# Subtracting the low halves of the layer weights on VectorE instead of GpSimd

## The chip, the cores and the metric

The kernel runs on one core of a Trainium2 chip. Times are device microseconds (us) of one execution. Before the change the median of three runs is 2853.03 us (2852.99 to 2853.11).

## The reference, cut to what matters

The program is a first block (pooling mixer, dilated attention, a 32-expert MoE) and then a second block, which goes through two layers on 256 tokens of width 1024. Only the second block is touched. One layer of it is:

```
x = x + 0.5 * swiglu(rms_norm(x, ffa_norm), ffa_w_in, ffa_w_out)
h = rms_norm(x, mix_norm)
(c_q, c_kv, k_rope, g_q, g_k, g_v, g_b, g_a, g_z, m_qkv, gate_logits) = split_cols(h @ w_in)
o_mla  = mla_branch(...)     # low-rank projections, head norms, rope, causal attention
o_gdn  = gdn_branch(...)     # causal convolution, l2 norm, gated delta rule
o_moba = moba_branch(...)    # head norms, rope, attention
up = einsum('bsnw,nwd->bsnd', stack(o_mla, o_gdn, o_moba), w_branch)
x = x + sum(sigmoid(gate_logits) * up, over the 3 branches) @ w_out
x = x + 0.5 * swiglu(rms_norm(x, ffb_norm), ffb_w_in, ffb_w_out)
```

## The kernel before

**Split weights.** Each matmul of a layer with a weight is three matmuls (`mm3`, L504 to L506): high part times high part, and the two mixed products. The high part of a weight is its copy rounded to the type fp32r, the low part is the weight minus that copy. A layer has 54 steps (`STEPS`), with one unit of weights each, and a unit comes as two "halves" (one for the last output step of each FFN), 106 halves in a layer. A half is cut into two pieces, mostly of 128x1024 values. For each piece SyncE loads 512 KB into one of four raw buffers, ScalarE writes the high part (`hi_act`, L483), GpSimd the low part (`lo_pool`, L489), and then the raw buffer is free for the load four pieces later. High and low parts lie in three slots of a half each. So ScalarE can start on half i only when TensorE has read half i-3 (`half_read`), and TensorE starts a half when both its low pieces are written (`weights`, semaphore `weights_split`).

**Who goes in which order.** Every engine runs a program written out by hand. ScalarE calls `splits.ahead(step)` at chosen places: it makes the high parts up to the third half after that step, so it waits there until TensorE is through with the step. GpSimd had nothing else to do in a layer, and wrote each low part as soon as its high part was there. VectorE does norms, rope, softmax, gates and the gated delta rule.

**TensorE's order in a layer:** norm transposes (L259); FFN 0; norm transposes; MLA rows; gates 0; transposes of the MLA latents (L1695); up_proj; gates 1; gates 2; MLA attention (L309 transposes q and k, L318 scores); MoBA rows 0 to 2; gates 3; gates 4; branch 0; MoBA attention; gdn 0 to 2; z; gates 5; l2 sums (L755); branch 2; the delta rule (L745); branch 1; wout 0 and 1; norm transposes; FFN 1. gates, gdn, branch and FFN-in steps are 96 matmuls of 256 columns, 48 to a half.

**VectorE's lines that matter:** head norms (L644, L645, L205, L206, a square root by ScalarE on L212, L647, L650 twice) and rope (L662 to L667, once for q and once for k) stand before each of the two attentions. `norm2_dve`: L205, L206, ScalarE's square root, L553 twice, then four parts of L559 and four times L562. The MLA latents go through L1815 and L1817. The branches' products are L1612. The convolution is L913 and L915, the l2 norm L923, L926, L930, L933. The merge of the branches is L1843 and L1847. ScalarE frees the PSUM banks of the gates with L1027, those of q, k and v with L1756 to L1762, and makes the products' banks of attention readable with L355.

Of the kernel before, what the change touches and what calls it, by code (L numbers as in the profile page):

```python
# [423 lines left out]
class Splits:  # L424
# [5 lines left out]
    def ahead(self, step):  # L430

        upto = min(last_half_of(step) + SPLIT_SLOTS + 1, len(HALVES))
        for i in range(self.done, upto):
            self.emit(self.k, self.eng, i)
        self.done = max(self.done, upto)
# [50 lines left out]
def lo_pool(k, pool, i):  # L486
    for n, at in pieces(i):
        pool.wait_ge(k.sem("weights_hi"), n + 1)
        k.nc.gpsimd.tensor_tensor(k.w[1][i % SPLIT_SLOTS][:, at], k.raw[n % RAW_SLOTS][:, 0:at.stop - at.start],  # L489
                                  k.w[0][i % SPLIT_SLOTS][:, at], ALU.subtract).then_inc(k.sem("weights_split"), 1)  # L490
# [56 lines left out]
def norm2_dve(k, dve, link, n, gain, power):  # L547
# [4 lines left out]
    for t in range(NT):  # L552
        V_.tensor_scalar(k.h[:, t, :], k.x[:, t, :], st[:, t:t + 1], None, ALU.mult).then_inc(k.sem("h_ready"), 1)  # L553
    for half in range(2):
# [63 lines left out]
def ffn_dve(k, dve, n):  # L618
    nc = k.nc
    silu, prod = k.s(SILU_TMP, 2, 512), k.s(SILU_TMP + 1024, 2, 512)  # L620
    for kind, u in FFN_STEPS:
        if kind == "out":
            continue
        b, free = k.filled(dve, ("up", n, u))
# [260 lines left out]
def gdn_dve(k, dve, link):  # L885
# [21 lines left out]
    for i in range(3):  # L907
        k.evacuated(dve, ("raw", i, 0), ("raw", i, 1))
        for j in range(4):
# [8 lines left out]
            else:  # L918
                ins.then_inc(k.sem("conv_ready"), 1)
    for i in range(2):  # L920
# [3 lines left out]
    for b4 in range(4):  # L924
        b, free = k.filled(dve, ("l2", b4))
        V_.tensor_scalar(G.sq[:, 2 * b4:2 * b4 + 2, :], part(b, 2, S), EPS, None, ALU.add).then_inc(free, 1)  # L926
    for b4 in range(4):
# [17 lines left out]
    link(V_.tensor_copy(G.XT[:, :].rearrange("p t h n -> p (t h) n"), bc(k.c("ident").unsqueeze(1), [P, 8, P])))  # L945
    branch_dve(k, dve, 2)
# [710 lines left out]
def layer_body(k, dram, layer):  # L1657
# [9 lines left out]
    with nc.Block() as block:  # L1667
# [124 lines left out]
        def _(dve):  # L1792
# [3 lines left out]
            norm2_dve(k, dve, link, 0, k.lv("g_ffa"), 0)  # L1796
            ffn_dve(k, dve, 0)
            norm2_dve(k, dve, link, 1, k.lv("g_mix"), 1)
            k.evacuated(dve, ("mla", 0), ("mla", 1))
# [10 lines left out]
            ins.then_inc(k.sem("c_ready"), 1)  # L1810
            gain = k.lv("c_norm")
# [12 lines left out]
            dve.wait_ge(k.sem("k_rope"), 2)  # L1824
            k.evacuated(dve, *[(x, t, i) for t in range(NT) for x in ("q", "kv") for i in range(2)])
            head_norm_dve(k, dve, link, mla.qk, k.s(QKT, 32, MLA_D), MLA_D, (k.lv("q_norm"), k.lv("k_norm")), 3)
            rope_dve(k, dve, link, mla.qk, QKT, 64, 16, k.c("cos16"), k.c("sin16"), k.sem("qk_ready"))
            mask = lambda t, pair: bc(causal[:, (1 - t) * P:2 * P].unsqueeze(1), [P, 2, (t + 1) * P])
            attn_dve(k, dve, link, mla, MLA_D ** -0.5, mask)
            k.evacuated(dve, *[("moba", i, t) for i in range(3) for t in range(NT)])  # L1830
            head_norm_dve(k, dve, link, moba.qk, k.s(QKT, 32, MOBA_D), MOBA_D, (k.lv("moba_q"), k.lv("moba_k")), 4)
            rope_dve(k, dve, link, moba.qk, QKT, 0, 32, k.c("cos32"), k.c("sin32"), k.sem("qk_ready"))
            branch_dve(k, dve, 0)
            attn_dve(k, dve, link, moba, MOBA_D ** -0.5, mask)
            gdn_dve(k, dve, link)

            branches = gatesT.rearrange("p (n c) s -> p n c s", n=3)
            link(V_.tensor_tensor(comb, branches[:, 0], branches[:, 2], ALU.add))
            branch_dve(k, dve, 1)
# [8 lines left out]
            for v in range(2):  # L1848
                for t in range(NT):
# [4 lines left out]
            ffn_dve(k, dve, 1)  # L1854

        @block.gpsimd
        def _(pool):
            for i in range(len(HALVES)):
# [174 lines left out]
```

## Time and profile before

| | |
|---|---|
| median of 3 runs | 2853.03 us |
| span of the profiled execution | 2852.2 us (0.8 us under the median) |
| TensorE busy | 2534.9 us, 89% |
| VectorE busy | 973.9 us, 34% |
| ScalarE busy | 888.3 us, 31% |
| GpSimd busy | 1027.5 us, 36% |
| first block | about 0 to 1170 us |
| layers | about 1170 to 2004 us and 2004 to 2852 us |

The span is the profiler's, from the first to the last instruction; the page gives no other time of that execution. The two layers are alike: the same TensorE stretches of the first layer lie 843 us earlier with durations equal to about 0.2 us, but for the first steps of either FFN and the MLA rows (11.40 us there, 9.47 here). Places are named by their time in the second layer.

### The profile page before, as it was taken

How to read it: one execution, taken by the hardware profiler on the slowest of the kernel's cores; microseconds unless marked ns; L12 is line 12 of the kernel's file. 1: busy time of each engine (PE TensorE's matmuls, PEld its weight loads, DVE VectorE, ACT ScalarE, POOL GpSimd, SP SyncE). 2: the span in 40 equal slices, each digit the busy share in tenths (PEclk: the TensorE clock that was granted, in tenths of full speed). 3: DMA queues.
4: the chain of work that ended last, by engine and by line, in shares of the span. 5: the costliest groups of instructions: out<-in, count | busy, mean ns of one | idle time of the engine just before them, and what ended most of it. 6: DMA issues, size and time to landing. Idle time of an engine off the chain costs nothing. (4 is left out here: it accounts for less than half of the span.)

```text
span 2852.2 us, 37927 instructions
## 1 busy us (share of the span) xinstructions
PE 2534.9 (89%) x15142; PEld 1826.0 (64%) x15142; DVE 973.9 (34%) x1514; ACT 888.3 (31%) x1266; POOL 1027.5 (36%) x428
## 2 busy tenths in 40 slices
PE   8889999999999998799778976899799777986899
PEld 3544443434434343599767866899799767875898
DVE  0322121212222121311465775221211557774221
ACT  1311212111111211444344531343444444431342
POOL 0000000000000000488548521688688546522686
PEclk9889999999999999899889997999899888997999
DMA  8249999999999995455325320354455324311453
GB/s 333 97 180 428 429 428 428 429 428 429 427 430 427 430 428 243 134 185 185 133 68 170 103 75 30 132 185 157 161 186 185 123 86 136 119 60 40 153 187 138
DMA packets 94236, 650.66 MB, mean 228 GB/s; under 512 B 10448, under 2 KB 12416, under 8 KB 68128
## 3 DMA queue, kind: packets, MB, share of 16 engines
q1 hardware_dynamic: 94112, 648.94, 58.8%
q8 instruction: 86, 1.41, 0.2%
q14 instruction: 38, 0.31, 0.0%
HBM read 647.84 MB, written 1.06 MB: 228 GB/s over the span
## 5 line engine op out<-in xcount | busy, mean ns | idle before, releaser
L489 POOL TENSOR_TENSOR w_lo<-raw,w_hi 128x1024 fp32r<-128x1024 f32 (+3 forms) x424 | 1027.3, 2446 | 1807.5 <-ACT w_hi L483 1807.5
L1319 PE MATMUL bank<-ring,scratch 128*64 128x512 f32 x3072 | 686.1, 596 | 27.2 <-DMA ring<-in_expert_units 25.4
L483 ACT CAST w_hi<-raw 128x1024 fp32r<-128x1024 f32 (+3 forms) x424 | 419.8, 1038 | 672.0 <-PE bank L506 659.6
L504 PE MATMUL bank<-hT_hi,w_hi 128*128 128x256 f32 x1984 | 566.1, 285 | 18.6 <-ACT scratch L1762 9.5
L505 PE MATMUL bank<-hT_lo,w_hi 128*128 128x256 f32 x1984 | 565.0, 285 | 0.0
L506 PE MATMUL bank<-hT_hi,w_lo 128*128 128x256 f32 x1984 | 564.9, 285 | 0.0
L1319 PEld LDWEIGHTS bank<-ring,scratch 128*64 128x64 f32 x3072 | 209.7, 137 | 455.0 <-issue 386.7
L504 PEld LDWEIGHTS bank<-hT_hi,w_hi 128*128 128x128 f32 x1984 | 384.8, 194 | 21.6 <-issue 10.5
L505 PEld LDWEIGHTS bank<-hT_lo,w_hi 128*128 128x128 f32 x1984 | 384.8, 194 | 0.8
L506 PEld LDWEIGHTS bank<-hT_hi,w_lo 128*128 128x128 f32 x1984 | 384.5, 194 | 0.0
L1487 DVE TENSOR_TENSOR scratch<-bank,scratch 128x512 f32<-128x512 f32 x64 | 44.3, 692 | 605.0 <-PE bank L1333 601.1
L626 DVE TENSOR_TENSOR scratch<-scratch,bank 128x512 f32<-128x512 f32 x44 | 30.3, 688 | 539.2 <-ACT scratch L612 539.2
L504 PE MATMUL bank<-w_hi,act_hi 128*128 128x512 f32 (+1 forms) x376 | 147.2, 392 | 6.9 <-ACT scratch L1027 6.9
L505 PE MATMUL bank<-w_lo,act_hi 128*128 128x512 f32 (+1 forms) x376 | 147.1, 391 | 0.0
L506 PE MATMUL bank<-w_hi,act_lo 128*128 128x512 f32 (+1 forms) x376 | 146.7, 390 | 0.0
L1305 PEld LDWEIGHTS bank<-scratch,h_rows 128*128 128x128 f32 x1056 | 124.9, 194 | 27.5 <-issue 27.5
L1305 PE MATMUL bank<-scratch,h_rows 128*128 128x128 f32 x1056 | 133.8, 281 | 0.0
L745 PE MATMUL bank<-scratch 128*128 128x128 f32 x816 | 106.0, 293 | 26.2 <-DVE scratch L986 7.3
L745 PEld LDWEIGHTS bank<-scratch 128*128 128x128 f32 x816 | 102.4, 206 | 32.0 <-issue 18.0
L1388 ACT COPY scratch<-bank 128x512 f32<-128x512 f32 x64 | 37.5, 586 | 265.9 <-PE bank L1319 265.9
L1390 ACT ACTIVATE scratch<-scratch 128x256 f32<-128x256 f32 x64 | 26.7, 417 | 276.2 <-DVE scratch L1490 276.2
L629 DVE TENSOR_TENSOR act_lo<-scratch,act_hi 128x512 fp32r<-128x512 f32 x44 | 102.3, 2324 | 30.2 <-ACT act_hi L615 30.2
(263 smaller groups left out, 2832.8 us busy)
## 6 DMA issues: line engine op xcount, KB each, us to landing
ring<-in_expert_units SPq DMA_DIRECT2D x192, 2048.0 KB, 20.5
raw<-in_layer_units SPq DMA_DIRECT2D x408, 512.0 KB, 4.7
ring<-in_first_units SPq DMA_DIRECT2D x6, 2048.0 KB, 23.9
ring<-in_ple_units SPq DMA_DIRECT2D x2, 2048.0 KB, 9.9
raw<-in_layer_units SPq DMA_DIRECT2D x8, 424.0 KB, 3.4
raw<-in_layer_units SPq DMA_DIRECT2D x4, 384.0 KB, 3.2
const<-in_const SPq DMA_DIRECT2D x1, 1184.0 KB, 7.3
x_res<-in_x SPq DMA_DIRECT2D x1, 1024.0 KB, 4.9
```

The lines of the kernel that those rows point to most:

```text
L483: k.nc.scalar.copy(k.w[0][i % SPLIT_SLOTS][:, at], k.raw[n % RAW_SLOTS][:, 0:at.stop - at.start]).then_inc(k.sem("weights_hi"), 1)
L489: k.nc.gpsimd.tensor_tensor(k.w[1][i % SPLIT_SLOTS][:, at], k.raw[n % RAW_SLOTS][:, 0:at.stop - at.start], k.w[0][i % SPLIT_SLOTS][:, at], ...
L504: nc.tensor.matmul(out, lhsT[0], rhs[0], start=start, stop=False)
L505: nc.tensor.matmul(out, lhsT[0], rhs[1], start=False, stop=False)
L506: return nc.tensor.matmul(out, lhsT[1], rhs[0], start=False, stop=stop)
L626: nc.vector.tensor_tensor(prod[:, u % 2, :], silu[:, u % 2, :], b[:, :], ALU.mult).then_inc(free, 1)
L629: nc.vector.tensor_tensor(lo, prod[:, u % 2, :], hi, ALU.subtract).then_inc(k.sem("act_lo"), 1)
L745: last = nc.tensor.matmul(b[:, h * P:(h + 1) * P], lhsT[:, h, :], rhs[:, h, :], start=True, stop=True)
L1305: last = nc.tensor.matmul(b[:, j * P:(j + 1) * P], k.h[:, t, c * P:(c + 1) * P], sel[:, t, :], start=(t == 0), stop=(t == 1))
L1319: last = nc.tensor.matmul(b[g * SL:(g + 1) * SL, :], lhsT[:, c, :], w[:, c, g, :], start=start and c == 0, stop=stop and c == 3)
L1388: nc.scalar.copy(rows[:, half, :], b[:, :]).then_inc(free, 1)
L1487: V_.tensor_tensor(both, b[:, :].rearrange("p (a n) -> p a n", n=SL), bc(wide_bias, [P, 8, SL]), ALU.add)\
```

## The change

The function `lo_pool` becomes `lo_dve`: the same subtraction, with the same semaphores, as a VectorE instruction. The GpSimd program of the layer goes. Since VectorE has an order of its own, its low parts are put into it at chosen places with `splits.ahead`, as ScalarE's are. The matmuls, the loads and ScalarE's program stay as they were.

```diff
     def ahead(self, step):
 
-        upto = min(last_half_of(step) + SPLIT_SLOTS + 1, len(HALVES))
+        self.to(last_half_of(step) + SPLIT_SLOTS + 1)
+
+    def to(self, end):
+
+        upto = min(end, len(HALVES))
         for i in range(self.done, upto):
             self.emit(self.k, self.eng, i)
         self.done = max(self.done, upto)
...
-def lo_pool(k, pool, i):
+def lo_dve(k, dve, i):
     for n, at in pieces(i):
-        pool.wait_ge(k.sem("weights_hi"), n + 1)
-        k.nc.gpsimd.tensor_tensor(k.w[1][i % SPLIT_SLOTS][:, at], k.raw[n % RAW_SLOTS][:, 0:at.stop - at.start],
+        dve.wait_ge(k.sem("weights_hi"), n + 1)
+        k.nc.vector.tensor_tensor(k.w[1][i % SPLIT_SLOTS][:, at], k.raw[n % RAW_SLOTS][:, 0:at.stop - at.start],
                                   k.w[0][i % SPLIT_SLOTS][:, at], ALU.subtract).then_inc(k.sem("weights_split"), 1)
...
         V_.tensor_scalar(k.h[:, t, :], k.x[:, t, :], st[:, t:t + 1], None, ALU.mult).then_inc(k.sem("h_ready"), 1)
+    between()
...
-def ffn_dve(k, dve, n):
+def ffn_dve(k, dve, n, splits):
...
         if kind == "out":
+            if u < FFN_OUT_UNITS - 1:
+                splits.ahead(STEP[f"ffn{n}", kind, u])
             continue
+        splits.ahead(STEP[f"ffn{n}", kind, u])
...
     for i in range(3):
+        splits.ahead(STEP["gdn", i])
         k.evacuated(dve, ("raw", i, 0), ("raw", i, 1))
...
+    splits.ahead(STEP["z", 0])
     for i in range(2):
         dve.wait_ge(k.sem("conv_silu"), i + 1)
...
         V_.tensor_scalar(G.sq[:, 2 * b4:2 * b4 + 2, :], part(b, 2, S), EPS, None, ALU.add).then_inc(free, 1)
+    splits.ahead(STEP["gates", 5])
...
     link(V_.tensor_copy(G.XT[:, :].rearrange("p t h n -> p (t h) n"), bc(k.c("ident").unsqueeze(1), [P, 8, P])))
+    splits.ahead(STEP["branch", 2])
     branch_dve(k, dve, 2)
...
+            splits = Splits(k, dve, lo_dve)
+            norm2_dve(k, dve, link, 0, k.lv("g_ffa"), 0, lambda: splits.to(1))
+            splits.to(SPLIT_SLOTS)
+            ffn_dve(k, dve, 0, splits)
             norm2_dve(k, dve, link, 1, k.lv("g_mix"), 1)
+            splits.ahead(STEP["ffn0", "out", 5])
+            splits.ahead(STEP["mla", 0])
...
             ins.then_inc(k.sem("c_ready"), 1)
+            splits.ahead(STEP["gates", 0])
...
+            splits.ahead(STEP["up_proj", 0])
             k.evacuated(dve, *[(x, t, i) for t in range(NT) for x in ("q", "kv") for i in range(2)])
             head_norm_dve(k, dve, link, mla.qk, k.s(QKT, 32, MLA_D), MLA_D, (k.lv("q_norm"), k.lv("k_norm")), 3)
+            splits.ahead(STEP["gates", 1])
             rope_dve(k, dve, link, mla.qk, QKT, 64, 16, k.c("cos16"), k.c("sin16"), k.sem("qk_ready"))
             mask = lambda t, pair: bc(causal[:, (1 - t) * P:2 * P].unsqueeze(1), [P, 2, (t + 1) * P])
+            splits.ahead(STEP["gates", 2])
             attn_dve(k, dve, link, mla, MLA_D ** -0.5, mask)
+            for i in range(3):
+                splits.ahead(STEP["moba", i])
             k.evacuated(dve, *[("moba", i, t) for i in range(3) for t in range(NT)])
             head_norm_dve(k, dve, link, moba.qk, k.s(QKT, 32, MOBA_D), MOBA_D, (k.lv("moba_q"), k.lv("moba_k")), 4)
+            splits.ahead(STEP["gates", 3])
             rope_dve(k, dve, link, moba.qk, QKT, 0, 32, k.c("cos32"), k.c("sin32"), k.sem("qk_ready"))
+            splits.ahead(STEP["gates", 4])
+            splits.ahead(STEP["branch", 0])
             branch_dve(k, dve, 0)
             attn_dve(k, dve, link, moba, MOBA_D ** -0.5, mask)
...
             link(V_.tensor_tensor(comb, branches[:, 0], branches[:, 2], ALU.add))
+            splits.ahead(STEP["branch", 1])
             branch_dve(k, dve, 1)
...
+                if v == 0:
+                    splits.ahead(STEP["wout", v])
...
             norm2_dve(k, dve, link, 2, k.lv("g_ffb"), 6)
+            splits.ahead(STEP["wout", 1])
+            ffn_dve(k, dve, 1, splits)
-
-        @block.gpsimd
-        def _(pool):
-            for i in range(len(HALVES)):
-                lo_pool(k, pool, i)
```

## Rows read from the trace of the kernel before

**Rows 1.** Busy time by stretch: us, then each engine's, clock, DMA; the mixing stretch

```profile
2215.00:2650.00 435.00, 340.98 (x2268) 310.72 (x2268) 265.38 (x323) 169.27 (x274) 201.77 (x81) 0.88 0.28 96
```

**Rows 2.** TensorE's waits in the second layer: us in total, times, longest

```profile
PE bank L309 <- DVE scratch L667: 26.4, 2, 14.1
...
PE bank L755 <- DVE scratch L923: 5.4, 1, 5.4
...
PE bank L504 <- ACT scratch L1027: 3.4, 1, 3.4
```

**Rows 3.** Costliest groups of the page: busy us, mean ns, idle before

```profile
L489 POOL TENSOR_TENSOR w_lo<-raw,w_hi 128x1024 fp32r<-128x1024 f32 (+3 forms) x424 | 1027.3, 2446 | 1807.5 <-ACT w_hi L483 1807.5
```

**Rows 4.** VectorE's groups by shape in the second layer

```profile
L629 DVE TENSOR_TENSOR act_lo<-scratch,act_hi 128x512 fp32r<-128x512 f32 x22 | 51.1, 2324 | 15.1 <-ACT act_hi L615 15.1
...
L923 DVE TENSOR_TENSOR scratch<-scratch 128x1024 f32<-128x1024 f32 x2 | 2.4, 1220 | 0.0
L1847 DVE TENSOR_TENSOR hT_lo<-scratch,hT_hi 128x512 fp32r<-128x512 f32 x4 | 2.5, 680 | 0.0
```

**Rows 5.** VectorE's timeline before MoBA attention: start, us, operation, idle before

```profile
2366.56 2.29 DVE L645 TENSOR_REDUCE scratch<-scratch 128x32 f32<-128x2048 f32 x1
...
2375.92 4.47 DVE L647 TENSOR_TENSOR scratch<-scratch 128x2048 f32<-128x2048 f32 x1 [4.33 <-ACT scratch L212]
...
2387.14 2.78 DVE L662 TENSOR_TENSOR scratch<-scratch,const 128x512 f32<-128x512 f32 x1
...
2403.82 0.69 DVE L662 TENSOR_TENSOR scratch<-scratch,const 128x512 f32<-128x512 f32 x1
...
2406.96 0.69 DVE L667 TENSOR_TENSOR scratch<-scratch 128x512 f32<-128x512 f32 x1
```

**Rows 6.** GpSimd's timeline in the same stretch

```profile
2379.30 23.94 POOL L489 TENSOR_TENSOR w_lo<-raw,w_hi 128x1024 fp32r<-128x1024 f32 x8 [1.05 <-ACT w_hi L483]
```

**Rows 7.** VectorE's timeline before MLA attention

```profile
2280.43 5.53 DVE L647 TENSOR_TENSOR scratch<-scratch 128x3072 f32<-128x3072 f32 x1 [5.37 <-ACT scratch L212]
...
2301.93 0.42 DVE L667 TENSOR_TENSOR scratch<-scratch 128x256 f32<-128x256 f32 x1
```

**Rows 8.** ScalarE's timeline: gates 2's banks freed before MLA attention

```profile
2290.27 1.08 ACT L1027 ACTIVATE scratch<-bank 128x512 f32<-128x512 f32 x2
```

**Rows 9.** Stretches with TensorE at either clock, columns as in Rows 1

```profile
2262.96:2268.90 5.94, 5.94 (x32) 5.94 (x33) 4.80 (x1) 1.00 (x4) 2.98 (x2) 0.59 0.65 228
2372.30:2395.35 23.05, 23.05 (x193) 22.84 (x191) 19.32 (x6) 12.74 (x15) 22.00 (x9) 1.00 0.54 179
```

**Rows 10.** DMA issues of the page: KB each, us to landing

```profile
raw<-in_layer_units SPq DMA_DIRECT2D x408, 512.0 KB, 4.7
```

**Rows 11.** VectorE's timeline at the start of the layer

```profile
2015.44 1.42 DVE L553 TENSOR_SCALAR h_rows<-x_res,scratch 128x1024 f32<-128x1024 f32 x2 [1.06 <-ACT scratch L212]
2017.40 0.69 DVE L559 TENSOR_TENSOR hT_hi<-bank,lvec 128x512 fp32r<-128x512 f32 x1 [0.54 <-PE bank L259]
```

**Rows 12.** VectorE's timeline after gates 0, around branch 2, the merge and norm 2

```profile
2245.75 0.56 DVE L1815 TENSOR_TENSOR act_hi<-bank,lvec 128x384 fp32r<-128x384 f32 x1 [3.47 <-PE bank L1695]
...
2504.37 12.98 DVE L930 RECIPROCAL scratch<-scratch 128x512 f32<-128x512 f32 x4
...
2525.13 2.49 DVE L1612 TENSOR_TENSOR scratch<-bank,scratch 128x512 f32<-128x512 f32 x4
...
2615.23 6.79 DVE L1843 TENSOR_TENSOR scratch<-scratch 128x512 f32<-128x512 f32 x4
...
2650.86 1.68 DVE L205 TENSOR_SCALAR scratch<-scratch 128x2 f32<-128x2 f32 x1 [3.42 <-ACT h_rows L233]
```

**Rows 13.** ScalarE's timeline at norm 1, after gates 0 and after the decay

```profile
2216.53 1.28 ACT L212 ACT_TABLE_LOAD   x1
...
2245.43 1.99 ACT L483 CAST w_hi<-raw 128x1024 fp32r<-128x1024 f32 x2 [4.19 <-PE bank L506]
...
2524.33 3.87 ACT L483 CAST w_hi<-raw 128x1024 fp32r<-128x1024 f32 x4
```

More of the change, by code:

```diff
@@ L542, in rows3_pe, with norm2_dve @@
             last.then_inc(k.sem("half_used"), 1)
-def norm2_dve(k, dve, link, n, gain, power):
+def norm2_dve(k, dve, link, n, gain, power, between=lambda: None):
     nc, st = k.nc, k.s(STATS, SCRATCH - STATS)
@@ L882, in gdn_act, with gdn_dve @@
         nc.scalar.copy(k.act2[0][:, 4:8, t * P:(t + 1) * P], part(b, 4, P)).then_inc(k.sem("go_hi"), 1)
-def gdn_dve(k, dve, link):
+def gdn_dve(k, dve, link, splits):
     nc, G = k.nc, Gdn(k)
@@ L1824, in _ @@
             dve.wait_ge(k.sem("k_rope"), 2)
+            splits.ahead(STEP["up_proj", 0])
             k.evacuated(dve, *[(x, t, i) for t in range(NT) for x in ("q", "kv") for i in range(2)])
             head_norm_dve(k, dve, link, mla.qk, k.s(QKT, 32, MLA_D), MLA_D, (k.lv("q_norm"), k.lv("k_norm")), 3)
+            splits.ahead(STEP["gates", 1])
             rope_dve(k, dve, link, mla.qk, QKT, 64, 16, k.c("cos16"), k.c("sin16"), k.sem("qk_ready"))
             mask = lambda t, pair: bc(causal[:, (1 - t) * P:2 * P].unsqueeze(1), [P, 2, (t + 1) * P])
+            splits.ahead(STEP["gates", 2])
             attn_dve(k, dve, link, mla, MLA_D ** -0.5, mask)
+            for i in range(3):
+                splits.ahead(STEP["moba", i])
             k.evacuated(dve, *[("moba", i, t) for i in range(3) for t in range(NT)])
             head_norm_dve(k, dve, link, moba.qk, k.s(QKT, 32, MOBA_D), MOBA_D, (k.lv("moba_q"), k.lv("moba_k")), 4)
+            splits.ahead(STEP["gates", 3])
             rope_dve(k, dve, link, moba.qk, QKT, 0, 32, k.c("cos32"), k.c("sin32"), k.sem("qk_ready"))
+            splits.ahead(STEP["gates", 4])
+            splits.ahead(STEP["branch", 0])
             branch_dve(k, dve, 0)
             attn_dve(k, dve, link, moba, MOBA_D ** -0.5, mask)
-            gdn_dve(k, dve, link)
+            gdn_dve(k, dve, link, splits)
             branches = gatesT.rearrange("p (n c) s -> p n c s", n=3)
             link(V_.tensor_tensor(comb, branches[:, 0], branches[:, 2], ALU.add))
+            splits.ahead(STEP["branch", 1])
             branch_dve(k, dve, 1)
@@ L1853, in _ @@
             norm2_dve(k, dve, link, 2, k.lv("g_ffb"), 6)
-            ffn_dve(k, dve, 1)
-        @block.gpsimd
-        def _(pool):
-            for i in range(len(HALVES)):
-                lo_pool(k, pool, i)
+            splits.ahead(STEP["wout", 1])
+            ffn_dve(k, dve, 1, splits)
     k.end_phase()
```

2 lines of the change are left out of this document (removed).

## The prediction

> **What bounds the kernel now.** I read the page first, then the busy time by stretch, the waits of TensorE, and the timelines of VectorE, ScalarE and GpSimd wherever TensorE stood still. TensorE sets the time. In the FFN stretches it never waits for a weight; in the mixing stretch of a layer it is busy for 341.0 of 435 us [rows 1], and what ends its longest pauses there is VectorE: 26.4 us of a layer wait for the rope that closes before the two attentions, 14.1 and so 12.3 us, then 5.4 us for the l2 squares [rows 2]. GpSimd is no bound by itself: it needs 2.446 us for a piece [rows 3], 4.9 us for a half, where a half of 48 matmuls takes 23.05 x 48/193 = 5.7 us [rows 9].
>
> But GpSimd slows VectorE. A rope multiply of 512 values takes 2.78 us while GpSimd works without a pause from 2379.30 to 2403.24, and 0.69 us at 2403.82 [rows 5, 6]. So do other operations with both inputs in SBUF: L647 with 2048 values takes 4.47 us where the one-input L645 with as many takes 2.29 [rows 5], and L629 takes 2.324 us for 512 values, where L1847 of the same shape and types takes 0.680 [rows 4]. These slow operations stand in the chains that TensorE waits for. The change removes GpSimd's work and so this excess. It adds 424 subtractions (two layers) to an engine with an order of its own, where a low part can be late, or the work behind it.
>
> **Prices.** The trace has no low part on VectorE. Below, it can't be under L1847's 0.680 us for half the values; above, it is 2.45 us if it cost what it does on GpSimd [rows 3, 4]. I take L923: 1024 values from SBUF, 1.22 us, the pair 2.35 [rows 4]; L1847 against 0.69 us in rope says that fp32r output costs nothing. A high pair is 1.99 us on ScalarE [rows 13], so after TensorE lets a slot go, the low pair ends 0.1 + 2.0 + 1.25 = about 3.4 us later on an idle VectorE (before: about 6). That keeps the FFN steps as they are: per step of two halves, 11.5 us, VectorE has two pairs and two small operations, some 6 us. The Trainium skill (VectorE: DVE Perf Modes, section on the TRN2 errata) has a table by which an fp32 operation of 1024 values takes 1.13 us; by that, an estimate, the nine or so pairs in the chains below would be 0.18 us shorter each, and the sum at the end 1.6 us lower per layer, 2848.4. The row of the trace decides, 1.22, and a second formula in that section gives the same.
>
> **Part by part, per layer** (plus is longer):
>
> - Layer start, +1.8. The first half's low pair stands between L553 and the first L559. It starts when L553 ends, 2016.86, ends at 2019.2, and L559 started at 2017.40 [rows 11]. TensorE waits for the third of the four parts that follow back to back.
> - Norm 1, -0.6; norm 2, -1.5. L205 took 1.68 us on 2 values beside GpSimd, and will take 0.17 as elsewhere. In norm 2 all of it shows [rows 12]; in norm 1 the square root's table load runs until 2217.81 anyway, and 0.6 is left [rows 13].
> - After gates 0, +2.3. The low pair of gates 1's first half is now ahead of L1815. Its high pair runs 2245.43 to 2247.42 [rows 13], the low pair ends at 2248.85, where L1815 started at 2245.75 [rows 12]: 3.1 later. TensorE waited for ScalarE's L1027 there in any case [rows 2], longer than for VectorE, which covers 0.8.
> - MLA rope, -4.2 before the clock. The square root comes at 2280.4 as before (ScalarE's order behind gates 1 sets it). From there L647 3.35, L650 2 x 1.7 (between 1024 and 2048 values): 2287.2. Then two low pairs until 2291.9, and rope 12 x 0.37 = 4.5: 2296.4, against 2302.35 [rows 7]. But TensorE needs the first of these pairs at 2282.6, for the second half of gates 2. It stands still for 7.0 us until 2289.7 and ends gates 2 at 2295.4, 7.1 late. Behind that wait are ScalarE's high pair for MoBA 1 (its raw buffers refill 4.7 us after the low pairs free them [rows 10], at 2295.4 and 2296.6) and then L1027, which frees the banks that attention needs first: it started at 2290.27 [rows 8] and will free the first bank at 2298.2. Attention starts at 2298.2 instead of 2302.4.
> - MoBA rope, -5.2 before the clock. The square root again comes as before, L647 at 2375.92 [rows 5]; 2.28 + 2.4 us bring the head norm to 2380.6. Two low pairs, 2385.3; rope 12 x 0.64 = 7.7, 2393.0 (before 2407.65 [rows 5]). TensorE wants gates 4's second half at 2378.1, gets it at 2383.0, wants branch 0's second half at 2394.5 and gets it at 2395.4. Branch 0 ends at 2401.2. Then gdn 1's first high pair and low pair (2404.5) stand before the L1612 quartet that frees the banks for k: 2407.0, the transposes end at 2407.8, and scores start at 2408.9, against 2414.1 now.
> - l2 and delta rule, +2.75. Two opposite terms. The convolution (two of three parts slowed) is no longer late, the 5.4 us wait [rows 2] goes; but two low pairs, 4.6 us, now stand before the reciprocals of 12.98 us [rows 12], and the sum there is only -2.2. After the decay, the low parts of the four high pieces of ScalarE (3.87 us, 2524.33 [rows 13]) come before L1612 at 2525.13 [rows 12]: the high ones now run from 2522.1 to 2526.0, the low ones follow from 2523.2, when VectorE's copies end, for 3 x 1.14 + 1.22 us, and L1612 starts at 2527.9. The chain behind it is one of latencies and moves whole.
> - Merge, +0.75. A low pair holds VectorE until 3.3 us after branch 1; then four L1612 (2.5, before mostly done while branch 1 ran) and L1843 in 2.5 instead of 6.79 [rows 12].
>
> The other places (MoBA rows, gdn steps, wout, FFN) cost nothing: the low pair is ready 3.4 us into a step of TensorE that lasts 11, and TensorE has a half or more in store; without that cover each would cost its 2.4 us. SyncE's loads wait for the low parts too. They start earlier than now where VectorE is free, and up to 7 us later in the two ropes, which is in the times above.
>
> **The clock.** TensorE resumes at half clock after each such pause: from 2262.96 the granted clock was 0.59 (between 1.2 and 2.4 GHz), 32 matmuls in 5.94 us where 3.8 would do, 2.1 lost [rows 9]. The new pauses of 7.0 and 4.9 us lie inside steps, so I charge 2.0 for MLA, 0.7 for MoBA (the 0.9 stall after it vanishes) and 0.5 after gates 0. The Trainium skill (TensorE: Matmul & The Clock Gate, section on HAM oscillation) has this as a rule that speaks against such a change: matmuls broken up by waits start slow again after each. The trace agrees, with 0.59 in that row.
>
> **Sum:** 1.8 - 0.6 - 1.5 + 2.3 - 4.2 - 5.2 + 2.75 + 0.75 = -3.9, with the clock +3.2: -0.7 per layer, -1.4 in all. The profiled span of 2852.2 us becomes 2850.8; the runs' median lies 0.8 above it, so 2851.6.
>
> **Rivals.** (1) Faster: the pauses are shorter or cost no clock, because high parts, loads and L1027 behind them come sooner than I chained them. With no clock term it is -3.9 per layer, 2845.2; with 1.5 us more from each rope, 2839. The overlap of operations and the bounds 0.68 to 2.45 allow it. (2) Slower: gates 2's late end. High pair, load and L1027 line up behind it, so that attention starts when it did, and MoBA likewise: the ropes' -9.4 + 2.7 go, +6.0 per layer, 2865. It decides when less than half of that gain (6.7) is left: then +2.6 per layer, 2858. Against it: L1027 has 4 us in hand. (3) A low part costs 2.4 us on VectorE too (L629's row read as the price of its types): about 1.2 us more for each of some 18 pieces in the chains, +21 per layer, 2893. L1847 speaks against it. (4) The change doesn't free VectorE: its slow operations have another cause. Then the low pairs come on top of the old chains, 4.7 us each at both ropes plus 9 elsewhere: about +18 per layer, 2889. The change from 2.8 to 0.69 us just when GpSimd stops speaks against it.
>
> **Chances.** Forecast, within 0.2% (5.7 us, about what a measurement tells from no change): 0.48. Rival 1: 0.28. Rival 2: 0.20. Rivals 3 and 4: 0.04. So faster 0.28, same 0.48, slower 0.24. The range reaches into rivals 1 and 2: 2841 to 2862; the forecast's own is 2847 to 2857.
>
> **What the profile would show.** Right: GpSimd empty after 1170 us; L489 on VectorE at 1.2 us; L662 to L667 at 0.4 and 0.7; L629 under 0.8; a TensorE pause of about 7 us in gates 2 and 5 us in gates 4, released by VectorE's low part; L309's pauses near 3 us and below; L755's pause gone; L1612 later after the decay. Wrong: a low part above 1.4 us, waits of TensorE for low parts in the FFN, or attention starting after 2302 minus the 1 us or so gained by then.

## The result and the profile after

The changed kernel took 2864.98 us (median of 5 runs, 2863.46 to 2866.44), the kernel before on the same chip 2853.11 us (2852.99 to 2855.46): a ratio of 1.004, 95% interval 1.0027 to 1.0052. It is slower, by more than the 0.2% that counts as no change, and outside the range of the prediction. In another set of runs, beside its own runs of the kernel before, it was 2863.46 us against 2854.37, ratio 1.0033 (1.0021 to 1.0046).

The page of the changed kernel: busy time of the engines, the costliest groups, the loads.

```profile
span 2863.1 us, 37969 instructions
...
PE 2561.6 (89%) x15142; PEld 1848.7 (65%) x15142; DVE 1238.8 (43%) x1938; ACT 891.4 (31%) x1266; POOL 0.2 (0%) x4
...
L493 DVE TENSOR_TENSOR w_lo<-raw,w_hi 128x1024 fp32r<-128x1024 f32 (+3 forms) x424 | 495.2, 1210 | 456.5 <-ACT w_hi L487 456.2
...
L508 PE MATMUL bank<-hT_hi,w_hi 128*128 128x256 f32 x1984 | 572.1, 288 | 46.3 <-DVE w_lo L493 24.7
...
raw<-in_layer_units SPq DMA_DIRECT2D x408, 512.0 KB, 4.9
```

GpSimd is empty, a low piece costs 1.21 us on VectorE, and VectorE is busy for 265 us more than before. TensorE is busy for 26.7 us more, with the same number of matmuls; its granted clock over the span is 0.936 instead of 0.942. The mixing stretch of the second layer, taken 7.7 us later here than in [rows 1], and TensorE's waits in it (in total, times, longest):

```profile
2222.70:2657.70 435.00, 352.80 (x2268) 321.14 (x2268) 279.68 (x401) 166.72 (x268) 0.00 (x0) 0.86 0.29 93
```

```profile
PE bank L508 <- DVE w_lo L493: 12.4, 2, 7.2
PE bank L508 <- DVE hT_lo L1873: 9.6, 1, 9.6
...
PE bank L753 <- DVE scratch L945: 5.0, 1, 5.0
...
PE bank L309 <- DVE scratch L1624: 3.0, 1, 3.0
PE bank L309 <- ACT scratch L1039: 3.0, 1, 3.0
```

The rope's 26.4 us of [rows 2] are gone and so are the 5.4 us of the l2 squares. In their place are two waits for a low part, 7.2 us in gates 2 and 5.1 in gates 4, and waits of 3.0 us at both attentions. VectorE's groups by shape in the second layer answer to [rows 4]:

```profile
L637 DVE TENSOR_TENSOR act_lo<-scratch,act_hi 128x512 fp32r<-128x512 f32 x22 | 15.2, 693 | 15.1 <-ACT act_hi L620 15.1
...
L933 DVE TENSOR_TENSOR scratch<-scratch 128x1024 f32<-128x1024 f32 x2 | 2.4, 1222 | 1.9 <-ACT scratch L867 1.9
...
L670 DVE TENSOR_TENSOR scratch<-scratch,const 128x512 f32<-128x512 f32 x2 | 1.4, 688 | 0.0
```

L637 is L629 of the kernel before, 0.693 us instead of 2.324. The rope operation that took 2.78 us beside GpSimd (L662 in [rows 5], L670 here) takes 0.69 us throughout; 1024 values from SBUF (L923, L933 here) take 1.22 us as before.

**Where the 10.9 us of span come from.** From the start of one TensorE stretch to the start of the next, second layer, changed minus before (us), beside the prediction's terms with its clock terms added where they fall (0.5 in up_proj, 2.0 and 0.7 in the two ropes):

| stretch | forecast | measured |
|---|---|---|
| layer start: transposes to FFN 0 | +1.8 | +1.65 |
| FFN 0 and norm 1 | -0.6 | -1.96 |
| norm 1's transposes to up_proj | +2.3 | +2.26 |
| up_proj to the end of MLA attention | -1.7 | -1.98 |
| MoBA rows to the end of MoBA attention | -4.5 | -0.94 |
| gdn steps to the first level of the delta rule | +2.75 | +2.94 |
| levels to wout | +0.75 | +0.87 |
| wout and norm 2 | -1.5 | -0.27 |
| FFN 1 and the end | 0 | +1.97 |
| **sum** | **-0.7** | **+4.54** |

The first layer is 3.9 us longer, and 2.5 us arise in the first block, before the layers. 3.9 + 4.5 + 2.5 = 10.9.

### The profile page after: what moved, and what is told of

It reads as the page before. It is cut to its first block and busy times, and to the rows that moved or that the text cites. A ratio compares the mean times of both kernels' runs of the same rounds, so it can differ in the third digit from the quotient of the medians.

```text
span 2863.1 us, 37969 instructions
## 1 busy us (share of the span) xinstructions
PE 2561.6 (89%) x15142; PEld 1848.7 (65%) x15142; DVE 1238.8 (43%) x1938; ACT 891.4 (31%) x1266; POOL 0.2 (0%) x4
## 5 line engine op out<-in xcount | busy, mean ns | idle before, releaser
L493 DVE TENSOR_TENSOR w_lo<-raw,w_hi 128x1024 fp32r<-128x1024 f32 (+3 forms) x424 | 495.2, 1210 | 456.5 <-ACT w_hi L487 456.2
L508 PE MATMUL bank<-hT_hi,w_hi 128*128 128x256 f32 x1984 | 572.1, 288 | 46.3 <-DVE w_lo L493 24.7
L1402 ACT ACTIVATE scratch<-scratch 128x256 f32<-128x256 f32 x64 | 26.7, 417 | 276.2 <-DVE scratch L1502 276.2
L508 PE MATMUL bank<-w_hi,hT_hi 128*128 128x512 f32 (+1 forms) x224 | 88.8, 396 | 22.2 <-DVE hT_lo L1873 19.2
L259 PE MATMUL bank<-const,h_rows 128*128 128x128 f32 x144 | 32.2, 416 | 77.4 <-DVE h_rows L557 53.0
```

The source lines that it names most:

```text
L259: last = nc.tensor.transpose(b[:, j * P:(j + 1) * P], k.h[:, t, c * P:(c + 1) * P], k.c("ident"))
L493: k.nc.vector.tensor_tensor(k.w[1][i % SPLIT_SLOTS][:, at], k.raw[n % RAW_SLOTS][:, 0:at.stop - at.start], k.w[0][i % SPLIT_SLOTS][:, at], ...
L508: nc.tensor.matmul(out, lhsT[0], rhs[0], start=start, stop=False)
L1402: nc.scalar.activation(sig[:, half], gu[:, half, :, 0:SL], ACT.Sigmoid, scale=ALPHA)\
```

## Why the attentions start so late

MLA attention first. VectorE's timeline, then ScalarE's, in the changed kernel (start, us, operation, idle before it and what ended it):

```profile
2289.22 3.36 DVE L655 TENSOR_TENSOR scratch<-scratch 128x3072 f32<-128x3072 f32 x1 [8.78 <-ACT scratch L212]
...
2296.20 4.63 DVE L493 TENSOR_TENSOR w_lo<-raw,w_hi 128x1024 fp32r<-128x1024 f32 x4
...
2304.81 0.42 DVE L675 TENSOR_TENSOR scratch<-scratch 128x256 f32<-128x256 f32 x1
```

```profile
2306.96 2.21 ACT L487 CAST w_hi<-raw 128x1024 fp32r<-128x1024 f32 x2 [1.45 <-DMA raw<-in_layer_units]
2309.07 1.08 ACT L1039 ACTIVATE scratch<-bank 128x512 f32<-128x512 f32 x2
```

The rope is through at 2305.2, but TensorE starts at 2309.80: the bank that it needs is freed by ScalarE's L1039, which stands behind a high pair, which waits for its load, which waited for the low pairs that were late. The pair isn't all of it: gates 2 ended only at 2306.80, behind the pause of 7.25 us in its middle, so without the pair L1039 could have started at most 2.3 us sooner. The same line forms before MoBA attention, and longer. VectorE, then ScalarE, then TensorE:

```profile
2387.16 4.63 DVE L493 TENSOR_TENSOR w_lo<-raw,w_hi 128x1024 fp32r<-128x1024 f32 x4
...
2399.31 4.62 DVE L493 TENSOR_TENSOR w_lo<-raw,w_hi 128x1024 fp32r<-128x1024 f32 x4
...
2411.50 2.44 DVE L493 TENSOR_TENSOR w_lo<-raw,w_hi 128x1024 fp32r<-128x1024 f32 x2 [2.03 <-ACT w_hi L487]
2413.85 2.48 DVE L1624 TENSOR_TENSOR scratch<-bank,scratch 128x512 f32<-128x512 f32 x4
```

```profile
2405.52 1.05 ACT L487 CAST w_hi<-raw 128x1024 fp32r<-128x1024 f32 x1 [4.22 <-DMA raw<-in_layer_units]
...
2410.42 1.05 ACT L487 CAST w_hi<-raw 128x1024 fp32r<-128x1024 f32 x1 [2.21 <-DMA raw<-in_layer_units]
...
2412.58 2.02 ACT L355 COPY scratch<-bank 64x512 f32<-64x512 f32 x4
```

```profile
2414.59 2.85 PE L309 MATMUL bank<-const,scratch 128*64 128x128 f32 x16 [3.04 <-DVE scratch L1624]
2418.31 10.58 PE L318 MATMUL bank<-scratch 64*128 64x128 f32 x32 [0.87 <-ACT scratch L355]
```

The two low pairs run until 2403.93, and each raw buffer is free only when its low piece ends, so ScalarE's high pieces come at 2405.52, 2407.16 and 2410.42, each after a wait for a load. VectorE's L1624, which frees the banks for the transposes, stands behind the last low pair, and ScalarE's eight L355, which the scores need, behind the last high pair. Then the 32 score matmuls run at the lower clock, in both layers. The clock of this and other stretches, changed kernel, then before (columns as in [rows 1]; the third value from the right is the granted clock):

```profile
2418.31:2428.89 10.58, 10.58 (x33) 8.62 (x34) 8.21 (x19) 6.68 (x25) 0.00 (x0) 0.50 0.04 16
...
2632.65:2657.22 24.57, 24.57 (x96) 19.77 (x96) 7.66 (x9) 6.01 (x6) 0.00 (x0) 0.89 0.26 85
2667.73:2716.01 48.28, 48.28 (x385) 48.28 (x386) 28.50 (x34) 18.83 (x21) 0.00 (x0) 0.95 0.58 186
```

```profile
2414.12:2419.59 5.47, 5.47 (x32) 4.67 (x32) 4.55 (x12) 4.42 (x18) 0.00 (x0) 1.00 0.01 1
2623.38:2646.71 23.33, 23.32 (x96) 18.87 (x96) 3.13 (x5) 6.01 (x6) 13.77 (x6) 0.94 0.31 105
2658.73:2705.04 46.31, 46.31 (x385) 46.31 (x386) 11.33 (x16) 18.70 (x21) 33.19 (x14) 1.00 0.44 143
```

The scores take 10.58 us at 0.50, the 1.2 GHz level, instead of 5.47 at 1.00; wout takes 1.24 us and the first part of FFN 1 1.97 us more, also at a lower mean clock. (In the first layer all of FFN 1 is only 0.8 us longer.)

The 5.1 us that the scores lose do not all reach the end of the attention. From their start to the next step (gdn 0) it takes 20.70 us in the changed kernel and 19.43 before, 1.27 more. Before, TensorE waited behind the scores for VectorE's softmax (L389), 0.47, 1.35, 1.26 and 1.10 us; in the changed kernel 1.00 us of such waits is left. The slow scores mostly fill time in which TensorE would have waited.

## Experiments

They ran in three sets, each beside runs of the kernel before on its own chip: 2854.65 us (median of 12 runs) for the first four, 2855.22 (21) for the next four, 2854.37 (16) for the last three. "After" stands for the changed kernel.

**1. The kernel before again.**

> The kernel before, unchanged, for a second profile. In the profile of the changed kernel the first block, which is not touched, ends 2.5 us later (the norm transposes of the first layer start at 1175.2 instead of 1172.7). If that is the scatter of the weight loads of the experts, two profiles of the same kernel differ there by some us too. If it belongs to the change, this profile shows 1172.7 again to within a few tenths.

Measured: 2853.65 us, span 2851.8; the transposes of the first layer start at 1172.8 us, 0.1 from the first profile. The trace of before repeats. By this expectation the 2.5 us would belong to the change; experiment 9 decides it the other way.

**2. The low pairs in the shadow of the head norms' square root.** VectorE waited 8.8 and 6.5 us there for ScalarE; the two low pairs now stand ahead of this wait.

```diff
 def rstd_dve(k, dve, link, v, mean, n, shadow=lambda: None):
...
     k.nc.vector.reciprocal(v, v).then_inc(k.sem("inverse_variance"), 1)
+    shadow()
...
-            head_norm_dve(..., 3)
-            splits.ahead(STEP["gates", 1])
+            head_norm_dve(..., 3, lambda: splits.ahead(STEP["gates", 1]))
```

and the same for `gates 3` in MoBA's head norm.

> Changed kernel, but the two low pairs that stood between head norm and rope are made while VectorE waits for the square root of the head norm, where it is idle for some 9 us. Theory 1 (place in VectorE's order): the pauses of 7.2 us in gates 2 and 5.1 us in gates 4 vanish, rope ends 4.7 us earlier in both, the gates keep 2.4 GHz; MLA attention starts about 9 us earlier and the MoBA scores about 8 us, some 17 to 22 us per layer: 2821 to 2831 us. Theory 2 (VectorE has 495 us more to do, wherever it stands, and TensorE's waits only move to another low part): less than 5 us in all, 2860 to 2865.

Measured: 2841.87 us, ratio 0.9953 (0.9940 to 0.9967). MLA attention starts 33.5 us behind up_proj's end instead of 42.6, and waits 3.6 us for the rope again. The stretch from the MoBA rows to the scores is 79.9 us against 84.0. MLA attention gains the 9 us expected, the MoBA scores 4 of the 8, and the whole is 23 us below after where 34 to 44 were expected. The reason is in TensorE's waits and in ScalarE's timeline:

```profile
PE bank L310 <- DVE scratch L1625: 4.7, 1, 4.7
PE bank L310 <- DVE scratch L676: 3.6, 1, 3.6
```

```profile
2389.77 1.04 ACT L488 CAST w_hi<-raw 128x1024 fp32r<-128x1024 f32 x1 [1.82 <-DMA raw<-in_layer_units]
...
2391.92 2.01 ACT L356 COPY scratch<-bank 64x512 f32<-64x512 f32 x4
```

The line of low pair, load, high pair and copies before MoBA attention is still there, with the scores at 10.58 us. The pauses inside gates 2 and 4, with what stands behind them, were worth 8.0 us per layer up to the end of MLA attention and 4.8 to 5.2 at MoBA, but they were not the only loss.

**3. TensorE kept busy in three pauses** (42, 56 and 38 products that nobody reads, before up_proj and before the second halves of gates 2 and 4).

```diff
+def keep_busy(k, pe, key, n):
+    k.evacuated(pe, key)
+    b, _ = k.uses.at[key]
+    for _ in range(n):
+        k.nc.tensor.matmul(k.bank[b][:, 0:S], k.hT2[0][:, 0, 0:P], k.hT2[0][:, 0, :], start=True, stop=True)
```

> Changed kernel, with added matmuls of 256 columns that nobody reads, put into three pauses of TensorE (42 after the latents' transposes, 56 before the second half of gates 2, 38 before that of gates 4), at 0.12 us each less than the pauses of 5.7, 7.2 and 5.1 us. Nothing else is changed. If the granted clock after a pause is what makes the change slower than forecast: up_proj falls from 9.4 to about 6.5 us, the half of gates 2 from 8.2 to 5.8, that of gates 4 from 8.0 to 5.8, 5 to 8 us per layer, 2849 to 2855 us. If the clock is beside the point: 2863 to 2867 us, since the pauses end when the low part is there.

Measured: 2861.88 us, ratio 1.0027 (1.0017 to 1.0038). up_proj takes 7.16 us (9.36 in after) and the halves behind the two pauses 6.01 and 6.02 us (8.2 and 8.7). So the three pauses cost 2.2 + 2.2 + 2.7 = 7.1 us of clock in the matmuls behind them in the second layer. But the layers are only 1.0 and 1.2 us shorter than in after. The time lies outside both expected ranges, 3.1 and 1.6 us under the two measurements of after, and the intervals of the ratios overlap. Up to the end of MoBA attention 2.5 of the 7.1 us arrive (3.5 in the first layer), and the stretch from the levels to wout, where nothing was edited, takes 2.7 us longer. TensorE's waits in the second layer:

```profile
PE bank L309 <- ACT scratch L1051: 5.3, 1, 5.3
PE bank L309 <- DVE scratch L1636: 4.8, 1, 4.8
```

These waits were 3.0 and 3.0 in after: TensorE arrives earlier and waits for ScalarE's and VectorE's line. Most of a pause's clock cost is hidden where another engine sets the next start.

**4. GpSimd busy again on its own data,** beside VectorE's low parts: the work of the change stays as it is, four subtractions of 256 values on GpSimd are added per high piece, and no one waits for them but the end.

```diff
+        @block.gpsimd
+        def _(pool):
+            link = chain_of(pool, k.sem("own_step"))
+            for n in range(2 * len(HALVES)):
+                pool.wait_ge(k.sem("weights_hi"), n + 1)
+                for _ in range(4):
+                    link(nc.gpsimd.tensor_tensor(k.fvec[:, 60:316], k.const[:, 0:256], k.const[:, 256:512], ALU.subtract))
```

> Changed kernel, with GpSimd busy again on values of its own: at each high piece it makes four subtractions of 256 values from constants into a table that the layers don't use. It shares no data with the rest and nobody waits for it. If GpSimd's work on SBUF is what made VectorE's operations with two SBUF inputs slow, they get slow again: rope of 512 values from 0.69 to more than 1.2 us, low parts from 1.21 to more than 1.8 us, and the time grows by more than 30 us, to over 2895. If the slowness had another cause, 2863 to 2867 us.

Measured: 3122.16 us, ratio 1.0932 (1.0911 to 1.0952). Of that, 72 us are GpSimd's own end: its work runs until 3116 us, TensorE's only until 3044, where it ended at 2857 in after. The rest is 187 us. It is no measure of what GpSimd cost before, since GpSimd is busy here for 1705.6 us and was for 1027.3. What bears on the question is VectorE's low part, whose data and order are unchanged:

```profile
L1891 POOL TENSOR_TENSOR fvec<-const 128x256 f32<-128x256 f32 x1696 | 1705.6, 1006 | 1410.3 <-ACT w_hi L487 1278.0
L493 DVE TENSOR_TENSOR w_lo<-raw,w_hi 128x1024 fp32r<-128x1024 f32 (+3 forms) x424 | 665.0, 1611 | 325.6 <-ACT w_hi L487 325.1
```

1.61 us in the mean against 1.21, and the rope multiply of 512 values (L670) 1.17 against 0.69. Both are slower, though not by as much as expected (over 1.8 and over 1.2). GpSimd's work slows VectorE's, as the prediction read it in [rows 5, 6], and rival 4 falls. The Trainium skill (SBUF — State Buffer, section on who interferes with whom) says that a VectorE instruction with two SBUF inputs contends with a GpSimd instruction that reads SBUF, and that one with at most one SBUF input doesn't, outside the modes in which it uses both ports, which copies and tensor_scalar can enter. These rows agree with it: the one-input reduction of 2048 values takes 2.29 us with GpSimd at work, here (L653) as in [rows 5] (L645), and 2.29 us in after, while the tensor_scalar L922 takes 0.88 us here and 0.35 in after.

**5. The low pair behind the latents.**

```diff
-            splits.ahead(STEP["gates", 0])
+            splits.to(last_half_of(STEP["gates", 0]) + SPLIT_SLOTS)
...                       (the latents' products)
+            splits.ahead(STEP["gates", 0])
```

> One place alone. The low pair of gates 1's first half goes behind the latent products, so that VectorE forms these as soon as gates 0 is through; only the pair of up_proj's second half stays ahead of them. If the pair standing ahead is what costs there (theory of order), the pause before the up projection goes from 5.66 us back to near 3.4 us and the up projection of 9.36 us to near 8.8 us: 2.8 us earlier in each layer, some 5.6 us in all, about 2859. The pause in gates 2 of 7.25 us stays or grows by what the lead was. Rival: the path behind it is held by ScalarE's high pieces and its copies of the banks, then attention starts when it did and nothing of the 2.8 us reaches the end: 2863 to 2866.

Measured: 2857.9 us, ratio 1.0009 (1.0000 to 1.0018). The pause before up_proj is 3.43 us and up_proj takes 8.75, as expected. Of TensorE's waits in the second layer the two that matter are both ScalarE's:

```profile
PE bank L508 <- ACT scratch L1039: 3.4, 1, 3.4
PE bank L309 <- ACT scratch L1039: 3.2, 1, 3.2
```

MLA attention starts 56.2 us behind the six transposes that follow gates 0 (58.4 in after): 2.2 of the 2.8 us arrive there. The layers are 1.8 and 3.5 us shorter in all, for other stretches moved too: in the second layer MoBA attention came out 2.9 us and FFN 1 2.0 us shorter, but the stretch from the levels of the delta rule to wout 2.5 us longer, none of which the edit touches. There the matmuls ran for 15.70 us at a granted clock of 0.54 behind the 320 of the levels, against 12.60 us at 0.68 (up to the matmuls of branch 1) in after.

**6. The low pairs around the delta rule moved off its chain.**

```diff
+    splits.to(last_half_of(STEP["gates", 5]) + SPLIT_SLOTS)
     for b4 in range(4):
+        if b4 == 2:
+            splits.ahead(STEP["gates", 5])
         b, free = k.filled(dve, ("l2", b4))
...
-    splits.ahead(STEP["gates", 5])
...
-    splits.ahead(STEP["branch", 2])
     branch_dve(k, dve, 2)
...                       (end of gdn_dve)
+    splits.ahead(STEP["branch", 2])
```

> The stretch from the l2 squares to the first level of the delta rule alone. The low pairs that stood ahead of the reciprocals and ahead of the copies of the branch product go behind them or between them. The stretch from the end of gates 5 to the first level took 44.67 us before and 47.61 us in the changed kernel. If the low pairs ahead of the chain are what costs (theory of order), 9.9 us of VectorE's work leave the chain in each layer: the stretch takes about 38 us, and the time is about 2845. Rival: ScalarE's part of the chain (its high pieces of 3.9 us and the decay) comes last, then the stretch takes 44 us or more and the time is 2858 or more.

Measured: 2845.73 us, ratio 0.9970 (0.9958 to 0.9981). From the end of gates 5 to the first level it takes 37.6 us (after 47.6, before 44.7; expected 38). VectorE's timeline in after, then in this kernel:

```profile
2503.38 4.62 DVE L493 TENSOR_TENSOR w_lo<-raw,w_hi 128x1024 fp32r<-128x1024 f32 x4
2507.92 12.98 DVE L941 RECIPROCAL scratch<-scratch 128x512 f32<-128x512 f32 x4
...
2529.01 4.63 DVE L493 TENSOR_TENSOR w_lo<-raw,w_hi 128x1024 fp32r<-128x1024 f32 x4 [0.37 <-ACT w_hi L487]
2533.56 2.48 DVE L1624 TENSOR_TENSOR scratch<-bank,scratch 128x512 f32<-128x512 f32 x4
```

```profile
2494.15 2.35 DVE L493 TENSOR_TENSOR w_lo<-raw,w_hi 128x1024 fp32r<-128x1024 f32 x2
...
2498.88 12.98 DVE L943 RECIPROCAL scratch<-scratch 128x512 f32<-128x512 f32 x4
...
2519.64 1.89 DVE L1626 TENSOR_TENSOR scratch<-bank,scratch 128x512 f32<-128x512 f32 x3
```

Both groups of four low pieces, 4.6 us each, stood in a chain of latencies, and the stretch is 10.0 us shorter in each layer, as expected. The median is 17.7 to 19.3 us under the two of after. The profiled execution, 2851.49 us and so 5.8 above the median, lost part of it again between the levels and wout, 2.7 us longer per layer, as in experiment 5.

**7. The branch products ahead of the low pairs** at MoBA attention (`branch_dve(k, dve, 0)` and `splits.ahead(STEP["branch", 0])` swapped on VectorE).

> Two lines swapped: VectorE forms the four branch products that free the banks for the k transposes of MoBA attention ahead of the low pair of branch 0's successor, not behind it. In the changed kernel TensorE pauses 3.04 us there and then takes 10.58 us for 32 score matmuls at the lower clock, where the kernel before took 5.48 us. If that pause is what lets the clock fall (theory of the clock), the pause goes to under 1 us, the scores take 5.5 to 8 us, and each layer gains 2 to 7 us: 2851 to 2861. Rival: the clock had fallen in the 5.11 us pause of gates 4 and does not come back in between; then the scores stay above 8 us, the gain is 0 to 2.4 us per layer, 2860 to 2865.

Measured: 2861.53 us, ratio 1.0025 (1.0014 to 1.0036). The pause before the transposes went, and one of 4.99 us came behind them, ended by ScalarE's L355; the scores stayed at 10.58 us and began 1.5 us earlier (82.6 us behind the rows). My theory that the pause at the transposes lets the clock fall is wrong as put: swapping VectorE's order only moves the pause, since the high pair ahead of L355 comes no sooner. The rival's range (2860 to 2865) held, but not its reason, that the clock doesn't come back after gates 4: the 32 transposes just before this pause ran in 3.65 us at a granted clock of 1.00.

**8. All placements together:** 2, 5, 6 and 7, and branch 1's low pair behind the merge.

> All placements together: low pairs in the shadow of the two head norms, behind the latents, behind the reciprocals and the decay, behind the branch products and behind the merge. The first of these alone measured 2841.9, 23 us under the changed kernel and 12.8 us under the kernel before on the same chip. If the places add up (theory of order), latents take 5.6 us, the delta stretch 19.8 us and the merge and the branch products some 3 to 8 us more from it: 2808 to 2814. Rival: what is taken from VectorE's order is then set by ScalarE or by the loads, and the places do not add: 2825 to 2840. Above 2842 the theory of order is wrong for all but the head norms.

Measured: 2797.71 us, ratio 0.9795 (0.9781 to 0.9808), lower than either theory had it. The places do add, 67 us below after (66 by its second measurement). Stretch by stretch of the second layer it is the sum of the single ones to about 1 us: -2.3 at the latents, -8.3 at MLA attention, -7.7 at MoBA attention (4.8 and 2.3 alone), -10.2 up to the levels. The rest is the pair at the merge, which was not tried alone: the pause before wout is 4.48 us instead of 9.62.

**9. The changed kernel again.**

> The changed kernel once more, for the scatter of its first block and a second profile. Theory: the extra 2.5 us of its first block (1175.2 us against 1172.6 to the first transposes of layer 1) belong to the expert loads and not to the change, since the four kernels that leave the first block alone showed 1173.2 to 1178.1; then the mixing stretches and the FFN repeat within 1 us and only the first block moves. The time comes to 2861 to 2866. Rival: the first block is again at 1175 or more and the time at 2865, as of an effect of the change.

Measured: 2863.46 us (2860.95 to 2869.46), span 2860.7. The first layer's transposes start at 1172.44 us (1175.18 in the first profile, 1172.65 in before). From there to those of the second layer 847.80 us (847.50; before 843.60), and from those to TensorE's end 833.93 (833.91; before 829.37). So the layers repeat to 0.3 us and their 8.4 to 8.8 us are the change's effect. The 2.5 us of the first block are not there again; the other kernels here that share after's first block had 1172.2 to 1178.1. It scatters from one execution to another, and I count it as that.

**10. One pair of each engine moved behind, before MoBA attention.** Only this, on after:

```diff
 ScalarE
-            splits.ahead(STEP["branch", 0])
-            attn_act(k, act, moba)
+            splits.to(last_half_of(STEP["branch", 0]) + SPLIT_SLOTS)
+            attn_act(k, act, moba, lambda: splits.ahead(STEP["branch", 0]))     (behind the eight L355)
 VectorE
-            splits.ahead(STEP["branch", 0])
             branch_dve(k, dve, 0)
-            attn_dve(k, dve, link, moba, MOBA_D ** -0.5, mask)
+            splits.to(last_half_of(STEP["branch", 0]) + SPLIT_SLOTS)
+            attn_dve(k, dve, link, moba, MOBA_D ** -0.5, mask, lambda: splits.ahead(STEP["branch", 0]))     (behind the softmax)
```

> The changed kernel with one pair of each engine moved: ScalarE makes the last high pair before MoBA attention behind its eight copies of the transposed q and k, and VectorE the low pair of it behind the softmax and the branch products ahead of it. In the changed kernel ScalarE's high pair at 2410.42 waits 2.21 us for its load and stands before these copies; the scores start at 2418.31, 84.04 us behind the start of the MoBA rows, and take 10.58 us. If the late low pair, the load behind it and the high pair behind that are what hold the scores (theory of the chain over three engines), the scores start some 80 us behind the rows and keep to 5.5 to 8 us: 4 to 9 us less per layer, 2848 to 2857. Rival: the copies are ready early but the clock is low anyway, 10.6 us for the scores, 2 to 4 us less per layer: 2857 to 2862.

Measured: 2853.17 us, ratio 0.9997 (0.9988 to 1.0006): no difference from the kernel before, 10 to 12 us below after. ScalarE and TensorE before the scores:

```profile
2404.96 3.96 ACT L355 COPY scratch<-bank 64x512 f32<-64x512 f32 x8 [1.74 <-PE bank L309]
2408.78 2.01 ACT L489 CAST w_hi<-raw 128x1024 fp32r<-128x1024 f32 x2
```

```profile
2404.32 3.65 PE L309 MATMUL bank<-const,scratch 128*64 128x128 f32 x32
2409.17 8.98 PE L318 MATMUL bank<-scratch 64*128 64x128 f32 x32 [1.19 <-ACT scratch L355]
```

The scores start 80.3 us behind the rows (84.0 in after, 80 expected) and take 8.98 us, a little over the 5.5 to 8 expected. From the rows to the end of this attention it is 98.7 us, against 104.7 in after and 105.7 before: 6.0 us for one pair on each engine, of which 3.8 are the earlier start of the scores. In the first layer it is 7.0 us, and the scores took 5.47 us there, behind the same pause:

```profile
1564.52 5.47 PE L318 MATMUL bank<-scratch 64*128 64x128 f32 x32 [1.19 <-ACT scratch L355]
```

**11. The same on top of all placements.**

> The same move on top of all the placements together, which measured 2797.7. There TensorE waited 4.85 us for ScalarE's first copy, and the scores took 10.57 us. By the chain over three engines the pause becomes about 1 us and the scores 5.5 us: 4 to 9 us less per layer, 2780 to 2790. Rival: the low pair behind the softmax comes too late for gdn 0's second half and gives it back: 2795 to 2802.

Measured: 2789.97 us, ratio 0.9775 (0.9762 to 0.9789). TensorE before the scores, in kernel 8 and then here:

```profile
2369.93 10.57 PE L319 MATMUL bank<-scratch 64*128 64x128 f32 x32 [4.85 <-ACT scratch L356]
```

```profile
2351.99 3.65 PE L310 MATMUL bank<-const,scratch 128*64 128x128 f32 x32
2356.83 5.47 PE L319 MATMUL bank<-scratch 64*128 64x128 f32 x32 [1.19 <-ACT scratch L356]
```

In the second layer both parts of what the line costs are gone: the pause is 1.19 us instead of 4.85, and the scores take 5.47 us instead of 10.57. In the first the scores still take 8.13 us:

```profile
1548.09 8.13 PE L319 MATMUL bank<-scratch 64*128 64x128 f32 x32 [1.47 <-ACT scratch L356]
```

That makes no difference to the end: the attention is over 18.8 us behind the start of the scores in the first layer and 18.9 in the second. With 10.57 us it was 21.2 and 19.7. This version is 2.25% faster than the kernel before and 2.6% faster than the change as made.

## Why the prediction was wrong

**The step that failed** is the MoBA rope, "-5.2 before the clock" with 0.7 for the clock. It was -0.94 instead of -4.5 by the end of that attention, 3.6 of the 5.2 us by which the second layer missed. It has two parts, 3.0 and 0.6 us:

- The line of engines. The prediction had "gdn 1's first high pair and low pair (2404.5)" ahead of the branch products, which end at 2407.0, and scores at 2408.9. The layer's part ahead of it runs 6.4 us later in after; less that, the low pair ended at 2407.5, the products at 2409.9 and the scores began at 2411.9, 3.0 late. Each raw buffer waits for a late low pair, and ScalarE then waited 4.22, 0.59 and 2.21 us for loads. I had named the mechanism for MLA and stopped short of pricing it here. This is the larger part: the sum let the last high and low pair follow at once, and had at nothing the waits for loads in front of them and the copies (L355) queued behind them.
- The clock. I took the scores to run at 2.4 GHz as before and even counted a stall as gone. They ran at 1.2 GHz, +5.1 us, of which 1.27 reached the end of the attention, since the softmax covers the rest; 0.7 was charged. Experiment 10 took out the pair that makes the line and had 6.0 us back, 3.8 by the earlier start and 2.2 within the attention.

**The clock elsewhere.** I charged 3.2 us per layer for it, at three pauses. Experiment 3 has 7.1 us of clock at these three, of which the 1.6 at up_proj were there before (8.75 us against 7.16): 5.5 are new. Too little charged, and yet not what moved the end, since little of what experiment 3 took away got there. What the forecast lacks are +1.97 us in FFN 1 and +1.24 in wout, and -1.3 in FFN 0. TensorE's pause before norm 2's transposes is 5.60 us in after and in experiments 5 and 6 alike, yet the first part of FFN 1 takes 48.28 us in the one and 46.31 in the other two. So these terms don't follow from the length of the pause; what they follow from no experiment shows, and they stay open.

**The total of rival 2.** Its 2865 us is what came. Its mechanism, "high pair, load and L1027 line up", is real at MLA attention, where the wait for L1039 (the same operation) comes last, but there the stretch still gained 1.98 us, where 1.7 was forecast. It decided at MoBA attention, and with other copies (L355 and not L1027). The chance of 0.20 was too low, since both ropes have the same line and I weighed only the first. And 2.5 us of the first measured time are the first block's scatter, so that the number agrees so well is luck.

**Right, term by term.** A low piece at 1.22 us (measured 1.221 for 1024 values); rival 3 falls. VectorE freed: L662's 2.78 us became 0.69 and L629's 2.324 became 0.693; experiment 4 puts the cause in GpSimd. Layer start +1.8 (1.65), latents +2.3 (2.26), the clock in up_proj +0.5 (0.62), delta rule +2.75 (2.94), merge +0.75 (0.87), norm 1 -0.6 (0.64). Norm 2's -1.5 was there (12.03 to 10.51 us) and was hidden by wout's clock. The pauses of 7.0 and 4.9 us in gates 2 and 4 were 7.25 and 5.11. MLA attention came right in part by luck: it started 1.6 us sooner behind up_proj's end, where 2.2 was forecast, and then was itself 1.0 us shorter, which the sum did not have.

The gain that a free VectorE offers was therefore there: experiments 2, 5, 6 and 10 each got some of it back by moving nothing but low or high pairs. The change lost it by placing low pairs (at MoBA attention a high pair of ScalarE's too, once it came late) ahead of the operation for which TensorE waits next.

## What to carry to other kernels

When work moves from a helper engine into the order of an engine on the critical path, each piece needs a place of its own: in the shadow of a wait that exists anyway, or behind the operation that TensorE needs next. One placement rule for all of them ("ahead of the next step") cost 75 us here against hand-picked places, one of them a high pair of ScalarE's. Where three engines feed a ring of buffers (load, high part, low part), follow a late piece once round the ring, load included, and through everything queued behind the next high part, before taking the gain of an earlier end for granted. And judge a placement by its own stretch, in both layers, and not by the total alone: the savings of the stretches added up to within about 1 us, while stretches that nobody touched moved by 2 to 3 us with the clock.

## What was not expected of the hardware

The clock of a stretch differed with the same work and the same idle before it, and between the two layers of one execution: 32 score matmuls behind transposes of 3.65 us and a pause of 1.19 us took 5.47 us in the first layer of experiment 10 and 8.98 in the second. The first part of FFN 1, whose norm transposes stand behind a pause of 5.60 us, took 46.30 us in the first layer of experiment 2 and 48.05 in the second. A pause is therefore not priced by its own length. The Trainium skill (TensorE: Matmul & The Clock Gate, section on what is actually happening) says that the number of matmuls at the low clock behind a start varies from run to run of one kernel; here it varied also between the layers of one execution, while two executions of the changed kernel agreed in the second layer (48.28 and 48.27 us). In the kernel before, the transposes of MoBA attention ran slowly behind 12.35 us of idle and the scores behind them at 2.4 GHz; in the changed kernel, behind pauses of 3.04 and 0.87 us, the scores ran at 1.2 GHz throughout.

GpSimd's subtraction of 256 values took 1.01 us in experiment 4, and four of them per high piece lengthened VectorE's low part by 0.40 us in the mean, although the two engines shared no data.
